# Product heads without GpSimd, last sums on TensorE, and the first root mean square inside the modulation stage

## What is computed

```python
def hybrid_layer(x, c, ...):                               # block 1
    mod = (silu(c) @ w_ada + b_ada)                        # shift1, scale1, gate1, shift2, ...
    h = rms_norm(x, norm1_g) * (1 + scale1) + shift1
    proj = h @ w_in
    ...
def second_block(x, c, ctx, ...):                          # block 2, for l in 0, 1
    o, oc = token_mixers(modulate(x, sh1, sc1), modulate(xc, sh1c, sc1c), w_in[l], ...)
    x = layer_norm(ALPHA * x + g1 * (o @ w_out[l]), ln1_g[l], ln1_b[l])
    x = layer_norm(ALPHA * x + g2 * swiglu(modulate(x, sh2, sc2), w_ffn_in[l], w_ffn_out[l]), ln2_g[l], ln2_b[l])
```

## Time and profile before

| | |
|---|---|
| median of 3 runs | 2734.43 us (2731.74 to 2739.71) |
| profiled execution, device time | 2729.32 us |
| its span | 2727.5 us |
| TensorE busy | 2360.7 us, 87% |
| VectorE busy | 915.5 us, 34% |
| ScalarE busy | 734.7 us, 27% |
| GpSimd busy | 174.8 us, 6% |
| issues of the start: tables, ctx | 1.16 us, 2.36 us |
| end of the last feed-forward product of layer 0, start of the next stage | 2175.4 us, 2179.2 us |
| mean granted clock of TensorE | 0.949 of full |

### The profile page before, as it was taken

How to read it: one execution, slowest core, us unless ns; L and a number is a source line. 1 busy time by engine, 2 the same in 40 slices (tenths; PEclk the granted TensorE clock), 3 DMA queues, 4 the chain that set the end, 5 groups by cost and what they waited for, 6 DMA issues and landing times. The chain is left out here.

```text
span 2727.5 us, 37039 instructions
## 1 busy us (share of the span) xinstructions
PE 2360.7 (87%) x14968; PEld 1563.6 (57%) x14968; DVE 915.5 (34%) x1592; ACT 734.7 (27%) x1216; POOL 174.8 (6%) x158
## 2 busy tenths in 40 slices
PE   4988898888888888888899877979999979877997
PEld 3956633333333333333388555658777779546997
DVE  1355311111111111111121655564344341647665
ACT  2345211111111111111042544342121242445333
POOL 0010000000000000000000213210000210112001
PEclk8978799999999999999999978989999989988998
DMA  8645699999999999999923332322331314424572
GB/s 255 176 139 188 232 380 386 387 387 387 387 387 387 387 387 387 387 387 387 376 72 120 124 109 94 108 73 78 104 93 63 100 56 136 139 93 122 150 192 80
DMA packets 449637, 605.51 MB, mean 222 GB/s; under 512 B 15056, under 2 KB 251600, under 8 KB 449392
## 3 DMA queue, kind: packets, MB, share of 16 engines
q1 hardware_dynamic: 449520, 603.84, 64.4%
HBM read 602.74 MB, written 1.05 MB: 221 GB/s over the span
## 5 line engine op out<-in xcount | busy, mean ns | idle before, releaser
L1860 PE MATMUL banks<-moe_ring,moe_x 128*64 128x512 f32 (+1 forms) x1920 | 346.3, 595 | 65.0 <-DMA moe_ring<-in_w_mlp 65.0
L1994 DVE TENSOR_SCALAR moe_glu<-banks 128x256 f32<-128x256 f32 x64 | 27.2, 424 | 872.2 <-PE banks L1860 872.2
L1860 PEld LDWEIGHTS banks<-moe_ring,moe_x 128*64 128x64 f32 (+1 forms) x1920 | 111.9, 126 | 295.2 <-issue 295.2
L2358 PE MATMUL banks<-ff_xhi,ff_whi 128*128 128x512 f32 (+1 forms) x672 | 226.6, 337 | 3.9 <-PEq L235 3.9
L2358 PE MATMUL banks<-ff_xhi,ff_wlo 128*128 128x512 f32 (+1 forms) x672 | 226.5, 337 | 0.0
L2358 PE MATMUL banks<-ff_xlo,ff_whi 128*128 128x512 f32 (+1 forms) x672 | 226.3, 337 | 0.0
L1935 ACT ACTIVATE moe_sig<-moe_glu 128x256 f32<-128x256 f32 x64 | 26.7, 417 | 627.4 <-DVE moe_glu L1994 627.4
L527 DVE TENSOR_TENSOR ff_wlo<-ring,ff_whi 128x2048 fp32r<-128x2048 f32 (+2 forms) x72 | 143.5, 1993 | 115.5 <-ACT ff_whi L518 113.4
L755 PE MATMUL banks<-pr_wlo,pr_xhi 128*128 128x256 f32 (+1 forms) x640 | 180.1, 281 | 0.0
L755 PE MATMUL banks<-pr_whi,pr_xlo 128*128 128x256 f32 (+1 forms) x640 | 180.0, 281 | 0.0
L755 PE MATMUL banks<-pr_whi,pr_xhi 128*128 128x256 f32 (+1 forms) x640 | 180.0, 281 | 0.0
(11 more groups left out here) (452 smaller groups left out, 4036.9 us busy)
## 6 DMA issues: line engine op xcount, KB each, us to landing
moe_ring<-in_w_mlp SPq DMA_DIRECT2D x256, 1024.0 KB, 14.2
ring<-in_w_mlp SPq DMA_DIRECT2D x128, 1024.0 KB, 14.2
ring<-in_w_ada SPq DMA_DIRECT2D x144, 512.0 KB, 4.7
ring<-in_w_ffn_in SPq DMA_DIRECT2D x88, 512.0 KB, 5.2
ring<-in_w_in SPq DMA_DIRECT2D x60, 512.0 KB, 5.0
ring<-in_w_ffn_out SPq DMA_DIRECT2D x48, 384.0 KB, 3.2
ring<-in_w_out SPq DMA_DIRECT2D x24, 512.0 KB, 4.3
ring<-in_w_ffn_out SPq DMA_DIRECT2D x16, 256.0 KB, 3.4
```

The source lines that it names most:

```text
L1860: mm = nc.tensor.matmul(out[o][c:c + n_cols, :], lhs[:, k, c:c + n_cols], self.moe_piece(4 * o + 2 * h + m)[:, k % 4, :], start=(o >= 4 an ...
L1994: nc.vector.tensor_scalar(g, u[:, 0, :], SWIGLU_LIMIT, None, ALU.min).then_inc(glus.sem, 1)
L2358: mm = nc.tensor.matmul(self.bank[2 * (f % 4) + side][:, 0:width], w[:, k, :], xp[:, k, :], start=(k == 0 and term == 0), stop=(k == KC - ...
```

## The change

In the heads GpSimd does nothing any more. VectorE splits the first weight chunk after the root products of the first two groups and takes the mean of the last group itself; the second weight chunk is rounded and split after the head. ScalarE rounds the first chunk at once, squares, and loads the table of the root after that. In the sums ahead of the projection of layer 1 and of the last norm, GpSimd leaves chunk 6 out (`added` = KC - 3) and TensorE adds it in the next stage: one more product for the sum and one for the squares. At the start only vectors and tables are waited for, behind them two ring chunks are issued; x, the other ring chunks and, last, ctx are issued in the modulation stage. The squares, their sums, the root and the products of the first norm are done there beside the modulation, and a short stage `modulate_rows` applies shift and scale on two engines.

```diff
@@ -540,15 +540,15 @@
             def _(sp):
                 self.load(sp, self.vecs[:, :], self.dram["vecs"])
                 self.load(sp, self.tables[:, :], self.dram["tables"])
-                self.load(sp, self.res[:, :, 0:S], self.dram["x"])
-                self.load(sp, self.res[:, :, S:2 * S], self.dram["ctx"])
-                self.refill(sp, SLOTS)
+                self.refill(sp, SLOTS // 2)
                 sp.wait_ge(self.loaded, self.n_loaded)
 
     def modulation(self, bias, chunks):
 
 
         nc = self.nc
+        total = self.bank[5][:, 0:S]
+        rstd = self.stat[:, 0, 0:S]
         nv, c, pair = 1, self.cond[:, :, 0:1], self.cond_pair[:, :, 0:2]
         src, src_pair = (self.vec(x).rearrange("p (k v) -> p k v", k=KC) for x in ("c", "cc"))
...
@@ -567,6 +567,12 @@
                 nc.scalar.activation(c, src, ACT.Sigmoid).then_inc(self.act_ready.sem, self.act_ready.one())
                 nc.scalar.activation(pair, src_pair, ACT.Sigmoid).then_inc(self.act_ready.sem, self.act_ready.one())
                 for i in range(chunks):
+                    if i == chunks - 1:
+                        act.wait_ge(self.dve_ready.sem, self.dve_ready.at(KC + 2))
+                        nc.scalar.activation(rstd, rstd, ACT.Ln).then_inc(self.act_step.sem, self.act_step.one())
+                        act.wait_ge(self.act_step.sem, self.act_step.count)
+                        nc.scalar.activation(rstd, rstd, ACT.Exp, scale=-0.5)\
+                            .then_inc(self.act_ready.sem, self.act_ready.one())
                     act.wait_ge(self.sums_ready.sem, self.sums_ready.at(i + 1))
                     nc.scalar.copy(line[:, i * CW:(i + 1) * CW], self.bank[i % 4][:, 0:CW])\
                         .then_inc(self.sums_taken.sem, self.sums_taken.one())
@@ -577,7 +583,17 @@
                 nc.vector.tensor_tensor(c, c, src, ALU.mult).then_inc(self.dve_ready.sem, self.dve_ready.one())
                 dve.wait_ge(self.act_ready.sem, self.act_ready.at(2))
                 nc.vector.tensor_tensor(pair, pair, src_pair, ALU.mult)
+                dve.wait_ge(self.rows_in.sem, self.rows_in.at(16))
+                for k in range(KC):
+                    nc.vector.tensor_tensor(self.h[:, k, S:2 * S], self.res[:, k, 0:S], self.res[:, k, 0:S], ALU.mult)\
+                        .then_inc(self.dve_ready.sem, self.dve_ready.one())
                 dve.wait_ge(self.pe_ready.sem, self.pe_ready.at(1))
+                nc.vector.tensor_scalar(rstd, total, 1.0 / D, EPS_RMS, ALU.mult, ALU.add)\
+                    .then_inc(self.dve_ready.sem, self.dve_ready.one())
+                dve.wait_ge(self.act_ready.sem, self.act_ready.at(3))
+                for k in range(KC):
+                    nc.vector.tensor_tensor(self.h[:, k, 0:S], self.res[:, k, 0:S], rstd, ALU.mult)
+                dve.wait_ge(self.pe_ready.sem, self.pe_ready.at(2))
                 b = self.vec(bias)[:, 0:2 * chunks].unsqueeze(2).to_broadcast([P, 2 * chunks, nv])
                 m = self.mod[:, :, :, 0:nv].rearrange("p i c v -> p (i c) v")[:, 0:2 * chunks, :]
                 nc.vector.tensor_tensor(m, out[:, 0:2 * chunks, :], b, ALU.add)
@@ -597,11 +613,42 @@
                         pe.wait_ge(self.sums_taken.sem, self.sums_taken.at(i))
                         for j in (2 * i - 2, 2 * i - 1):
                             mm = self.row_turn(out[:, j, :], line[:, P * j:P * j + P], nv)
+                    if i in range(chunks - 5, chunks - 1):
+                        for k in (2 * (i - chunks + 5), 2 * (i - chunks + 5) + 1):
+                            pe.wait_ge(self.dve_ready.sem, self.dve_ready.at(k + 2))
+                            sq = nc.tensor.matmul(total, self.tab("ones")[:, 0:P], self.h[:, k, S:2 * S],
+                                                  start=(k == 0), stop=(k == KC - 1))
+                        if i == chunks - 2:
+                            sq.then_inc(self.pe_ready.sem, self.pe_ready.one())
                 mm.then_inc(self.pe_ready.sem, self.pe_ready.one())
 
             @block.sync
             def _(sp):
-                self.refill(sp, chunks)
+                sp.dma_start(self.res[:, :, 0:S], self.dram["x"]).then_inc(self.rows_in.sem, 16)
+                self.refill(sp, chunks + SLOTS // 2)
+                self.load(sp, self.res[:, :, S:2 * S], self.dram["ctx"])
+
+    def modulate_rows(self, gain, shift, scale):
+
+        nc = self.nc
+        with self.stage() as block:
+            @block.vector
+            def _(dve):
+                nc.vector.scalar_tensor_tensor(
+                    self.amp[:, :], self.mod[:, scale, :, 0], 1.0, self.vec(gain), ALU.add, ALU.mult)\
+                        .then_inc(self.dve_ready.sem, self.dve_ready.one())
+                for k in range(1, KC, 2):
+                    if k == 1:
+                        dve.wait_ge(self.dve_ready.sem, self.dve_ready.at(1))
+                    nc.vector.tensor_scalar(self.h[:, k, 0:S], self.h[:, k, 0:S], self.amp[:, k:k + 1],
+                                            self.mod[:, shift, k, 0:1], ALU.mult, ALU.add)
+
+            @block.scalar
+            def _(act):
+                act.wait_ge(self.dve_ready.sem, self.dve_ready.at(1))
+                for k in range(0, KC, 2):
+                    nc.scalar.activation(self.h[:, k, 0:S], self.h[:, k, 0:S], ACT.Identity,
+                                         bias=self.mod[:, shift, k, 0:1], scale=self.amp[:, k:k + 1])
 
...
                 if head:
-                    self.head_scalar(act, head, x, width, highs)
+                    self.head_scalar(act, head, x, width, lambda act: self.split_high(act, bufs, n, 0))
                 else:
-                    highs(act, 0)
+                    self.split_high(act, bufs, n, 0)
                     self.input_high(act, x, width)
                 at = -1
                 for g, (i, (c0, c1), kind, place, t, n_tok) in enumerate(groups()):
                     if i != at:
                         at = i
-                        if i + 1 in nth and not (head and i == 0):
-                            highs(act, i + 1)
+                        if i + 1 in nth:
+                            self.split_high(act, bufs, n, i + 1)
                         if head and head["norm"] and i < KC:
                             self.head_residual(act, head, i, width)
                     act.wait_ge(self.sums_ready.sem, self.sums_ready.at(g + 1))
...
             @block.vector
             def _(dve):
-                if head:
-                    self.head_vector(dve, head, x, width, lambda dve, i: self.split_low(dve, bufs, n, i, i + 1))
-                    dve.wait_ge(self.lo_ready.sem, self.lo_ready.at(2))
                 for i in nth:
-                    if not (head and i < 2):
-                        self.split_low(dve, bufs, n, i, nth[i])
-                    if i == 0 and not head:
+                    if i == 0 and head:
+                        self.head_vector(dve, head, x, width, lambda dve: self.split_low(dve, bufs, n, 0, 1))
+                        continue
+                    self.split_low(dve, bufs, n, i, nth[i])
+                    if i == 0:
                         self.input_low(dve, x, width)
 
             if clear:
...
-        add(high, high, r(KC - 2)).then_inc(step.sem, step.one())
-        add_square(KC - 2)
+        if added == KC - 2:
+            pool.wait_ge(self.res_ready.sem, self.res_ready.at(KC - 1))
+            pool.wait_ge(step.sem, step.count)
+            add(high, high, r(KC - 2)).then_inc(step.sem, step.one())
+            add_square(KC - 2)
         pool.wait_ge(step.sem, step.count)
         pool.wait_ge(self.squares_added.sem, self.squares_added.count)
 
-    def norm_tensor(self, pe, width):
+    def norm_tensor(self, pe, width, added):
 
 
         nc, ones = self.nc, self.tab("ones")[:, 0:P]
         total, spread = self.bank[6][:, 0:width], self.bank[7][:, 0:width]
-        nc.tensor.matmul(total, ones, self.stat[:, 0, 0:width], start=True, stop=False)
-        nc.tensor.matmul(total, ones, self.res[:, KC - 1, 0:width], start=False, stop=True)\
-            .then_inc(self.norm_summed.sem, self.norm_summed.one())
+        mm = nc.tensor.matmul(total, ones, self.stat[:, 0, 0:width], start=True, stop=False)
+        for k in range(added + 1, KC):
+            mm = nc.tensor.matmul(total, ones, self.res[:, k, 0:width], start=False, stop=(k == KC - 1))
+        mm.then_inc(self.norm_summed.sem, self.norm_summed.one())
         nc.tensor.matmul(spread, ones, self.h[:, 0, 0:width], start=True, stop=False)
+        for k in range(added + 1, KC - 1):
+            nc.tensor.matmul(spread, ones, self.h[:, k, 0:width], start=False, stop=False)
         pe.wait_ge(self.squared.sem, self.squared.at(1))
         nc.tensor.matmul(spread, ones, self.h[:, KC - 1, 0:width], start=False, stop=True)\
...
         if head["norm"]:
-            self.norm_tensor(pe, width)
```

(54 more changed lines are left out.)

29 lines of the change are left out of this document (10 added, 19 removed).

## The result

The changed kernel takes 2694.68 us (median of 4 runs, 2692.75 to 2695.86) against 2737.07 us for the kernel before in the same series (2731.74 to 2742.34): ratio 0.9844, 95% interval 0.9822 to 0.9867. In a second series it took 2699.57 us (2698.48 to 2701.96) against 2734.11, ratio 0.9875 (0.9859 to 0.9892). It is faster by 35 to 42 us; forecast was 35. The two medians of the changed kernel are 4.9 us apart themselves, so the gain is known no better than that. The profiled executions took 2729.32 and 2695.86 us, 33.5 apart.

A forecast was written before the change was run, and what follows sets the result against it. TensorE, busy 2360.7 of 2727.5 us, was taken to wait where one chain runs alone, in the heads and start. Terms summed to -35.0: 2729.3 to 2694.3 profiled, 2699.4 with the median's 5.1 offset; range 2689 to 2714.

The forecast's parts named there:

- Case 6: Whole kernel: the outcome as forecast, 2694 to 2704 us; chance 0.59.
- start: First loads, modulation and first root mean square: -11.5 us, between -14.6 and -8.
- head with no norm: Second block's first head: cast and split of the second chunk leave the front, -1.85 us.
- head A: First groups of the first layer's feed-forward, whose input is normalised first: -8.4 us.
- sums ahead and head B: Late sums, then first groups of the second layer's projection, whose input is normalised first: together -7.9 us.
- head C: First groups of the second layer's feed-forward, whose input is normalised first, width 256: -4.4 us.
- end: Last norm: two GpSimd additions go, two 128x256 products come on TensorE, -0.95 us.
- Rival 3: Start hidden better, modulation's tail bounds and not SyncE, added splits lie beside ScalarE; 2692 us; chance 0.15.
- Rival 4: VectorE's long passes do not come from GpSimd; the three normed heads keep their time; 2728 us; chance 0.04.
- Rival 1: In the heads, VectorE's stall behind GpSimd's first instruction has another cause and stays; 2706 to 2710 us; chance 0.07.
- Rival 5: Slower: TensorE's clock stays at half in long product stages behind the heads; about 2775 us; chance 0.03.

The follow-up runs named there:

- the tighter start: Changed kernel with square sums and root one chunk earlier and ctx issued a stage later; 2694.29 us, one run.
- sums put back: Changed kernel with GpSimd's last two additions put back in all three places; 2704.39 us, ratio 0.9884.
- gaps: Kernel before, with GpSimd's second and third instruction in the normed heads each waiting on a semaphore for the one before; 2732.95 us.
- clears beside the same passes: Changed kernel with twelve GpSimd clears of an unused spare tile in the first stage of each feed-forward part; 2700.38 us.
- additions on unrelated tiles: Changed kernel with nine GpSimd additions of 128x512 into an unused spare tile in the first stage of each feed-forward part; 2713.2 us.
- the kernel with the loads alone: Kernel before with only the new order of the first loads; root mean square stage and heads as before; 2738.47 us.
- leaving one split: Changed kernel with the first weight split of each normed head put back on GpSimd; 2700.53 us, one run.

## Why the prediction was right, and where it was not

Forecast 2699.4 us, 2689 to 2714; measured 2694.68 and 2699.57. Case 6, as forecast. The shifts put the terms side by side:

| step | forecast | measured |
|---|---|---|
| start | -11.5 | -11.05 |
| head with no norm | -1.85 | -1.81 |
| head A | -8.4 | -8.50 |
| sums ahead and head B | -7.9 | -7.87 |
| head C | -4.4 | -4.38 |
| end | -0.95 | -1.55 |
| sum | -35.0 | -35.16 |
| stretches between, same code | 0 | +1.70 |

**Start.** The view that counted was SyncE's issues: ctx ended its issue at 44.16 (forecast 43.7), the last sums began at 38.48 (37 to 38.5), the cast came at 47.52 (47). Two things in the sum were off without showing in it. The square sums ended at 38.55 and not between 35.6 and 37.5, so VectorE's tail of the root ended at 44.08 and not by 43.1; that SyncE still bounds is a matter of 0.08 us. And the 5.33 us of rows 15 are not eight products at the half clock: the granted clock reads 0.50 up to 48, 0.74 from 48 to 50 and 1.00 behind. Two square products at the half rate took 2.05 us in the changed kernel, at the full 1.11, where I had 1.33. The last of the modulation's row sums took 1.07 us instead of 1.93, so the clock was full there, as I had taken it to be. Rival 3 (hidden better) is what the tighter start shows.

**Head A** was right term by term: -10.34 up to the root passes (10.35), +1.91 from there to the last split (+1.8), 0.03 for the second chunk (0.1).

**Head B**, by its first instruction: the stage starts 2.54 us earlier relative to mark 2150 (-2.5), the root passes 8.69 (-8.9), then +1.92 (+1.95) and +1.34 (+1.4 to 1.5). My 5.5 us from start to variance was 5.5. In it I had the price of two products, 1.5 to 1.7 us, and no number for the first products, which I called slow. Both are there: 1.7 for the four records more, 1.5 back because TensorE starts at the full clock. I had not seen that the late sums themselves bring the clock. One row I misread: the addition at 2177.17 is GpSimd's last and ends at 2178.42 itself; the first of the two started at 2175.95. The 2.1 us taken from there is right.

**Head C**: -4.06 to the root passes (-4.1), -2.27 to the last split (-2.2), +1.86 for the second chunk (+1.9).

**End**: the last norm begins 1.36 us earlier (-1.4) and its first sums give 0.43 back (0.45), so the late sums are worth 0.93, as forecast. The other 0.62 is TensorE's clock again, which my sum left out. In the first trace of before it falls during this norm's sums (granted 0.50 from 2715 to 2717), and the last two records start 0.59 us apart; in the first of the changed kernel it reads 1.00, and they start 0.22 apart. It stayed full in seven of the eight traces with the late sums and in two of the six without (sums put back, gaps). In the second trace of the changed kernel it fell, and the shift steps by +0.63. How much of this belongs to the change stays open.

**The cause.** Rival 4 is out: clears beside the same passes cost nothing, additions on unrelated tiles 5.3 us. Rival 1, that only the first instruction's part is GpSimd's, is out by the forecast's own outcome (0.43 us left). Its rule is sound, VectorE can get in behind the first instruction (3.99 us in the kernel with the loads alone), but what I drew from it was not: the rest needs no other cause, since the passes behind wait for GpSimd's next instructions and the head is only 0.6 us shorter. What I had as "VectorE stood still" is narrower: passes that read PSUM went on. Rival 5 is out: the mean granted clock is 0.957 after and 0.949 before.

**What I did not see** is that the recorded execution of before was a lucky one. I added the 5.1 us between it and its median to the forecast as a plain offset; 4.1 of it is the routing's step, which 12 of the 14 profiled executions have. The terms of the sum were right to 0.2 us; that the total fell on its number too is in part luck, since the stretches with the same code moved by -2.5 to +3.6 us each. The first trace after has it, so its -33.5 understates the change by about 4, and the medians (42 and 35 us) bracket it. The +1.70 between the stages is the sum of such steps: +3.55 up to 1362 us, +2.13 from there to head A, -2.52 in the first layer's feed-forward, +0.02 to head C, -1.48 in the last feed-forward. In the feed-forward the granted clock dips at the boundaries of its parts, 0.91 in one 20 us window of before and 1.00 in the one after:

```profile
1985.00:2005.00 20.00, 18.65 (x75) 15.31 (x76) 7.97 (x9) 4.29 (x3) 0.00 (x0) 0.91 0.39 106
```
```profile
1969.00:1989.00 20.00, 18.06 (x80) 15.01 (x81) 8.57 (x10) 4.30 (x3) 0.00 (x0) 1.00 0.39 109
```

Whether the new heads make these dips rarer stays open: seven of nine traces with changed heads won 1.7 to 2.6 us between marks 1811 and 2150, the other two 0.2 and 0.3, and the four with the old heads (besides the first of before) at most 0.5.

## What to carry to other kernels

A long pass of VectorE in a chain that runs alone is read together with what GpSimd does in the same microseconds: if both go SBUF to SBUF and the ends coincide, try taking the help away; here leaving one split or spacing the three gave less or nothing. A pause ahead of TensorE can cost more than its own length: see at which clock the products behind it run. Before moving a load, see whether the stage ends with the transfer, with the queue that issues it, or with an engine. And before explaining 4 us between two traces, compare stretches whose code is the same: they showed here that 4.1 us of it was chance.
